# Sparse attention loop: scores five blocks ahead in four PSUM banks, and four buffers of weights

## The reference

```python
logits = jnp.einsum('bthc,btjc->bthj', qb, kv_sel) * (KV_LATENT ** -0.5)
bias = jnp.moveaxis(rel_bias[bucket], -1, 2)
logits = logits + bias.astype(jnp.float32)
logits = jnp.where(valid[:, :, None, :], logits, -jnp.inf)
p = jax.nn.softmax(logits, axis=-1).astype(x.dtype)
o = jnp.einsum('bthj,btjc->bthc', p, kv_sel)
```

## Time and profile before

| What | us |
|---|---|
| median of 3 runs | 3218.07 |
| profiled execution | 3217.28 |
| its span | 3215.4 |
| busy TensorE matmul | 2917.2 (91%) |
| busy VectorE | 1410.9 (44%) |
| busy ScalarE | 920.1 (29%) |
| busy GpSimd | 608.5 (19%) |

### The profile page before, as it was taken

How to read it: one execution, slowest core, us unless ns; L and a number is a source line. 1 busy time by engine, 2 the same in 40 slices (tenths; PEclk the granted TensorE clock), 3 DMA queues, 4 the chain that set the end, 5 groups by cost and what they waited for, 6 DMA issues and landing times.

```text
span 3215.4 us, 42405 instructions
## 1 busy us (share of the span) xinstructions
PE 2917.2 (91%) x17555; PEld 2265.1 (70%) x17555; DVE 1410.9 (44%) x2428; ACT 920.1 (29%) x1696; POOL 608.5 (19%) x534
## 2 busy tenths in 40 slices
PE   8999999999999999999997988888698897988884
PEld 7659999998888778887875555555576674555552
DVE  5635323343345543234444543332597744533234
ACT  4544313233223342232222111111336621211111
POOL 2404101120011220012001432222000003522220
PEclk9999999999999999999998999999899998999997
DMA  4012232222222222222216999999421119999996
GB/s 138 27 53 80 79 105 80 92 79 70 79 70 79 79 78 98 95 96 79 92 53 258 395 409 409 409 408 390 151 88 47 50 60 383 406 409 409 409 409 267
DMA packets 272212, 600.31 MB, mean 187 GB/s; under 512 B 32647, under 2 KB 177602, under 8 KB 255626
## 3 DMA queue, kind: packets, MB, share of 16 engines
q1 hardware_dynamic: 247552, 569.47, 47.1%
q0 software_dynamic: 23968, 27.93, 2.7%
q10 hardware_dynamic: 490, 0.08, 0.0%
HBM read 607.75 MB, written 39.89 MB: 201 GB/s over the span
## 4 chain that ended last, share of the span: by engine, by line
PE 82%; DVE 7%; DMA 4%; issue 4%; ACT 2%; SPq 1%; POOL 1%; ACTq 0%; DVEq 0%; POOLq 0%
PE ps L101 76%; PE ps L104 5%; DMA sb_ring<-in_exp_w_dram 1%; DVE sb_tmpA L118 1%; DVE sb_arena L126 1%; DMA sb_hx<-in_exp_w_dram 1%; DMA sb_arena<-in_exp_w_dram 1%; DVE sb_ws L118 1%; SPq L144 1%; DVE sb_tmpA L126 1%; DVE sb_arena L118 1%; POOL sb_arena L118 0%; DMA sb_arena<-x_rows,sb_smallu 0%; DVE sb_tmpA L2204 0%; DVE sb_tmpA L122 0%
## 5 line engine op out<-in xcount | busy, mean ns | idle before, releaser
L101 PE MATMUL ps<-sb_hs,sb_ws 128*128 128x264 f32 (+1 forms) x6384 | 1106.7, 335 | 17.2 <-ACT sb_hs L108 7.5
L101 PEld LDWEIGHTS ps<-sb_hs,sb_ws 128*128 128x128 f32 x6384 | 971.3, 190 | 148.0 <-issue 16.5
L118 DVE TENSOR_TENSOR sb_ws<-sb_ring,sb_ws 128x1024 fp32r<-128x1024 f32 x279 | 370.6, 1333 | 429.1 <-ACT sb_ws L112 428.6
L101 PE MATMUL ps<-sb_arena 128*64 128x256 f32 (+14 forms) x2052 | 376.5, 429 | 36.7 <-issue 29.7
L112 ACT CAST sb_ws<-sb_ring 128x1024 fp32r<-128x1024 f32 x279 | 290.9, 1046 | 333.0 <-PE ps L101 318.1
L101 PE MATMUL ps<-sb_ring,sb_arena 128*64 128x256 f32 (+2 forms) x2314 | 318.6, 430 | 57.5 <-issue 53.8
L101 PE MATMUL ps<-sb_br,sb_ws 128*128 128x264 f32 (+1 forms) x2304 | 367.4, 321 | 0.0
L101 PEld LDWEIGHTS ps<-sb_br,sb_ws 128*128 128x128 f32 x2304 | 332.4, 188 | 34.2 <-issue 0.5
L101 PEld LDWEIGHTS ps<-sb_arena 128*64 128x64 f32 (+4 forms) x2052 | 220.5, 158 | 154.2 <-issue 88.3
L101 PEld LDWEIGHTS ps<-sb_ring,sb_arena 128*64 128x64 f32 (+1 forms) x2314 | 192.5, 146 | 149.4 <-issue 85.9
L108 ACT ACTIVATE sb_arena<-ps 64x256 f32<-64x256 f32 (+6 forms) x188 | 73.8, 403 | 780.9 <-PE ps L101 758.3
(11 more groups left out here) (189 smaller groups left out, 2265.1 us busy)
## 6 DMA issues: line engine op xcount, KB each, us to landing
sb_ring<-in_exp_w_dram SPq DMA_DIRECT2D x160, 1024.0 KB, 21.2
sb_hx<-in_exp_w_dram SPq DMA_DIRECT2D x128, 1024.0 KB, 21.5
sb_arena<-in_exp_w_dram SPq DMA_DIRECT2D x96, 1024.0 KB, 21.3
sb_ring<-in_mlp_w_dram SPq DMA_DIRECT2D x64, 1024.0 KB, 5.1
sb_ring<-in_od_w_in_dram SPq DMA_DIRECT2D x24, 1024.0 KB, 5.3
sb_ring<-in_conv_w_in_dram SPq DMA_DIRECT2D x12, 1024.0 KB, 5.0
sb_ring<-in_attn_w_in_dram SPq DMA_DIRECT2D x10, 1024.0 KB, 5.2
sb_ring<-in_od_w_out_dram SPq DMA_DIRECT2D x8, 1024.0 KB, 4.8
```

Source lines behind the costliest of these rows:

```text
L101: return self.e.matmul(o, l, r, start=start, stop=stop, skip_group_check=True)
L118: return self.e.tensor_tensor(o, a, b, op)
```

## The change

TensorE gets a ring of four banks for scores (0, 1, 6 and 7) and makes the scores of block x + 5 in step x. VectorE makes scores and maximum of block x + 3, and ScalarE its exponent, in step x, while reciprocal, scaling, transposes and copy still belong to x + 1 and the product to x. The weights get four separate buffers, places 0, 1, 2 and 5 of `tmpA` (3 and 4 stay `PTd`), and `soft_cols` four sets. The loops of ScalarE and VectorE start at x = -3 as before, TensorE's at -5.

```diff
-        P, PTd = tmpA[:, 0:3, 0:512], tmpA[:, 3:5, 0:512]
+        PB, PTd = [tmpA[:, i, 0:512] for i in (0, 1, 2, 5)], tmpA[:, 3:5, 0:512]
...
-            kb, tb, ob = (Ring([BANK[i], BANK[i + 1]], U_, emptied) for i in (0, 2, 4))
-            for x in range(-3, 64):
-                if x + 3 < 64:
-                    h, r = (x + 3) // 4, (x + 3) % 4
+            kb = Ring([BANK[i] for i in (0, 1, 6, 7)], U_, emptied)
+            tb, ob = (Ring([BANK[i], BANK[i + 1]], U_, emptied) for i in (2, 4))
+            for x in range(-5, 64):
+                if x + 5 < 64:
+                    h, r = (x + 5) // 4, (x + 5) % 4
                     n = 128 * (r + 1)
-                    u = kb.take(e, ("ds", x + 3))
+                    u = kb.take(e, ("ds", x + 5))
...
-                        q = e.tp(u[:, 128 * j:128 * j + 128], P[:, (x + 1) % 3, 128 * j:128 * j + 128], ident)
+                        q = e.tp(u[:, 128 * j:128 * j + 128], PB[(x + 1) % 4][:, 128 * j:128 * j + 128], ident)
...
-                if 0 <= x + 2 < 64:
-                    r = (x + 2) % 4
-                    p = P[:, (x + 2) % 3, 0:128 * (r + 1)]
-                    mx, den, inv = soft_cols(x + 2)
-                    e.wait_ge(*dve_dsa["max", x + 2])
+                if x + 3 < 64:
+                    r = (x + 3) % 4
+                    p = PB[(x + 3) % 4][:, 0:128 * (r + 1)]
+                    mx, den, inv = soft_cols(x + 3)
+                    e.wait_ge(*dve_dsa["max", x + 3])
...
-            c = 192 + 4 * (x % 3)
+            c = 192 + 4 * (x % 4)
...
-                    e.wait_ge(*scored["dsa", x + 2])
+                    e.wait_ge(*scored["dsa", x + 3])
                     e.wait_ge(*tb_in[h % 4][h])
-                    if x + 2 >= 3:
+                    if x + 3 >= 4:
                         e.wait_ge(*turned["dp", x - 1])
...
-                    p = P[:, (x + 1) % 3, 0:128 * ((x + 1) % 4 + 1)]
+                    p = PB[(x + 1) % 4][:, 0:128 * ((x + 1) % 4 + 1)]
```

More of the change, by code:

```diff
@@ L2030, in dsa_pe @@
                     e.mm(u[:, 0:n], oT[h][:, 128 * r:128 * r + 128], ckvT[:, 0:n], True, True).then_inc(
-                        *scored.mark(("dsa", x + 3)))
+                        *scored.mark(("dsa", x + 5)))
                 if 0 <= x + 1 < 64:
@@ L2098, in dsa_act @@
             for x in range(-3, 64):
-                if 0 <= x + 2 < 64:
-                    r = (x + 2) % 4
-                    p = P[:, (x + 2) % 3, 0:128 * (r + 1)]
-                    mx, den, inv = soft_cols(x + 2)
-                    e.wait_ge(*dve_dsa["max", x + 2])
-                    e.act(mx, mx, ACT.Identity, scale=-1.0).then_inc(*act_dsa.mark(("less", x + 2)))
-                    e.wait_ge(*act_dsa["less", x + 2])
-                    e.act(p, p, ACT.Exp, bias=mx, acc=den).then_inc(*act_dsa.mark(("exp", x + 2)))
+                if x + 3 < 64:
[3 more added lines that the diff above has]
+                    e.wait_ge(*dve_dsa["max", x + 3])
+                    e.act(mx, mx, ACT.Identity, scale=-1.0).then_inc(*act_dsa.mark(("less", x + 3)))
+                    e.wait_ge(*act_dsa["less", x + 3])
+                    e.act(p, p, ACT.Exp, bias=mx, acc=den).then_inc(*act_dsa.mark(("exp", x + 3)))
                 if 0 <= x + 1 < 64:
@@ L2191, in dsa_dve @@
                     split_lo(e)
-                if 0 <= x + 2 < 64:
-                    h, r = (x + 2) // 4, (x + 2) % 4
+                if x + 3 < 64:
+                    h, r = (x + 3) // 4, (x + 3) % 4
                     n = 128 * (r + 1)
-                    p = P[:, (x + 2) % 3, 0:n]
-                    mx, den, inv = soft_cols(x + 2)
-                    e.wait_ge(*scored["dsa", x + 2])
+                    p = PB[(x + 3) % 4][:, 0:n]
+                    mx, den, inv = soft_cols(x + 3)
+                    e.wait_ge(*scored["dsa", x + 3])
                     e.wait_ge(*tb_in[h % 4][h])
-                    if x + 2 >= 3:
+                    if x + 3 >= 4:
                         e.wait_ge(*turned["dp", x - 1])
-                    e.stt(p, U_["ds", x + 2][:, 0:n], SC128, backwards(TB[:, h % 4, 0:n]), ALU.mult, ALU.add).then_inc(
-                        *dve_emptied.mark(("ds", x + 2)))
-                    e.wait_ge(*dve_emptied["ds", x + 2])
+                    e.stt(p, U_["ds", x + 3][:, 0:n], SC128, backwards(TB[:, h % 4, 0:n]), ALU.mult, ALU.add).then_inc(
+                        *dve_emptied.mark(("ds", x + 3)))
+                    e.wait_ge(*dve_emptied["ds", x + 3])
                     e.e.tensor_tensor_reduce(p, p, madd[:, r, 0:n], 1.0, SENT, ALU.add, ALU.max, mx).then_inc(
-                        *dve_dsa.mark(("max", x + 2)))
+                        *dve_dsa.mark(("max", x + 3)))
                 if 0 <= x + 1 < 64:
-                    p = P[:, (x + 1) % 3, 0:128 * ((x + 1) % 4 + 1)]
+                    p = PB[(x + 1) % 4][:, 0:128 * ((x + 1) % 4 + 1)]
                     mx, den, inv = soft_cols(x + 1)
```

## The result

The changed kernel takes 3195.85 us (median of 4 runs, 3194.71 to 3196.09), beside 3218.34 us for the kernel before: a ratio of 0.993, with a 95% interval of 0.9912 to 0.9947. The profiled execution took 3195.65 us, its span is 3193.9.

What follows compares the result with a forecast made beforehand. Bound: VectorE and TensorE taking turns in the steady loop, 7.15 us a head. Savings of 18.2 us over 14 laps, 1.5 at the start and 2.0 at the end, together 21.7 off 3218.07, gave 3196.4; range 3191 to 3208.

Steps and rivals of the forecast that it cites:

- The bound: Steady loop before: VectorE and TensorE take turns, 7.15 us a head; TensorE's transposes of r=2 wait 1.3 us for scaled weights.
- VectorE's own time, 5.72: Steady loop: what VectorE needs for one head if it never waits, 7.15 us less idle time, reciprocal's wait and overlaps.
- TensorE's own time, 5.68: Steady loop: what TensorE needs for one head if it never waits, 5.46 us plus 0.22 for the last pair.
- The ring through ScalarE, 5.74: Once a head: product r=3, output copy, exponent, copy r=1, product r=1; 2.94 us on ScalarE's side, 2.80 on TensorE's.
- 5.85 a head: Steady loop after the change: 5.74 us plus three hand-offs of about 0.04, bounds 5.74 and 6.3.
- Rival B: Steady loop: limits don't mesh, each block pays a 0.14 us hand-off, 6.3 a head, 3203.2 us; chance 0.18.
- Rival C: Loop and its start: 5.74 us a head and a start at full clock, 3193.4 us; chance 0.12.
- The start, 1.5 between 0 and 3: Start of the loop: 1.5 us saved, as block 3's scores come before TensorE's idle time, at full clock.
- The end, 2.0: End of the loop: the last two outputs copied 4.7 us apart instead of 6.67, saving 2.0 us.
- What follows keeps the gain: After the loop: projection and expert weights move with the loop's end, so nothing swallows the 21.7 us.
- The bias tiles: GpSimd's loads for head h+4: land 1.9 to 5.0 us after issue, needed 17 us later, so hidden.
- rival E: Loop: slower, TensorE's clock stays at 1.2 GHz from the start on, 11.2 us a head, 3279 us; chance 0.04.

Runs made afterwards that it cites:

- e2: The changed kernel with two score banks instead of four and scores made four blocks ahead instead of five: 3211.25 us, ratio 0.998.
- e1: The kernel before with only TensorE's part of the change, four score banks and scores five blocks ahead: 3205.62 us, ratio 0.9963.
- e11: The changed kernel with its four score banks kept but scores made four blocks ahead: 3208.91 us in one run.
- e4: The changed kernel with ScalarE's copy of a head's output moved behind the next step's exponent and copy: 3192.94 us, ratio to before 0.9924.
- e12: The changed kernel with scores made six blocks ahead instead of five, in the same four banks: 3195.86 us in one run, 5.71 us a head.
- e6: The changed kernel with VectorE's two weight splits made before the loop instead of in steps 0 and 1: 3191.68 us, ratio to before 0.9922.
- e3: The changed kernel with three weight buffers instead of four: 3238.0 us, ratio 1.0066.

## Why the prediction was right

- **The bound.** Right. The chain of before was this ring: e2, which leaves one block between making and reading scores as it was, keeps it at 6.85 us. That its 1.3 us of TensorE's idle time come from scores "just made" is borne out by e1, which moves scores alone and takes 0.80 off a head and leaves 0.7 of the 1.3, and by e11, in which banks without distance take nothing off e2's head. The sign that TensorE's waits for the scaling fall below 0.1 us holds for its matmul rows, which show none, but weight loads still wait up to 0.3 us for it.
- **VectorE's own time, 5.72.** Right to 0.01: e4 and e12 both settle at 5.72 a head with only VectorE in their chains. Subtracting idle time and then the overlaps of unwaited successors was worth the trouble; without the overlaps it would have been 6.0.
- **TensorE's own time, 5.68.** Too high by 0.2, without consequence. It was added up from transposes that had waited, and those handed TensorE on later than unwaited ones: two, three and four of them after 0.28, 0.39 and 0.50 us in the rows of before, and after 0.21, 0.33 and 0.43 without a wait. After the change the head is 5.79, less the 0.19 that product r=1 starts late and the 0.11 that it then takes longer: 5.49. So VectorE and the ring lay close together, TensorE did not.
- **The ring through ScalarE, 5.74.** Right in its path, and to 0.04 in size: 2.94 on ScalarE's side as added up, 2.84 instead of 2.80 on TensorE's. There two differences cancel in part. Product r=1 waits now and hands on after 0.55 us (2473.84 to 2474.39; 0.44 before), and the transposes of r=3 don't wait now and hand on after 0.43 (0.50 before). Shown by taking pieces out of it in two places (e4 the output copy, e12 two units of scores), each of which brought the head to VectorE's time.
- **5.85 a head.** 0.06 too much: three hand-offs of 0.04 were added to the ring, and it came out 0.04 above its sum. Times 14 that is, with the shorter last lap, the 1.0 us by which the middle of the loop beat the forecast. Rival B (each block pays 0.14) didn't come: in 2450 to 2480 VectorE shows no wait for TensorE at all. Rival C (5.74 and a full clock) lay nearer in the head than the forecast, but its clock fell.
- **The start, 1.5 between 0 and 3.** 1.9, inside the bounds; that it lies near the middle is luck, for 1.5 was taken without terms of its own. The clock fell later and for less time: the change's clock is 0.69 in 2424 to 2426, 0.50 in 2426 to 2428 and 0.96 in the next two; that of before is 0.56 in 2422 to 2424, 0.50 to 2432 and 0.88 behind it. That scores are made ahead of the idle time, that the second scaling comes later (0.27 us for the 0.35 added up) and that TensorE has little to do until then (2.17 us idle) were seen beforehand. What I did not ask is why the two splits stand there, while VectorE idles for 6 us ahead of the loop: e6 has 3 us from it.
- **The end, 2.0.** 1.8, with 4.86 between the last two outputs for 4.7.
- **What follows keeps the gain.** Right: the first expert weights are issued 23.73 us earlier (2614.74 for 2638.47), the loop's gain of 22.9 and the 1.0 by which it began earlier, less 0.2. Of the 2.4 us that the two profiles lose behind it, the medians show little (0.4).
- **The bias tiles.** Right: nobody waits for them, with 3.4 us to landing.
- **The rules weighed.** By the rule of the Trainium skill (Perfetto Trace Analysis, Optimization Strategy) that consistent bubbles can mean too few buffers, the head would have gone to TensorE's 5.68. The trace after agrees with the place, the 1.31 us are gone; the head stays 0.11 above that figure because the ring sets it. And buffers alone did nothing here: e11 with four banks and e2 with two both take 6.85 us a head, until scores are made one block further ahead. The rule of the Trainium skill on cycling through PSUM banks (TensorE: Matmul & The Clock Gate, A second HAM failure mode: psum-queue depth-cycling), which stood for rival E, is not borne out: with eight banks in rotation the granted clock of the steady loop is 1.00.

## What to carry to other kernels

Where engines hand blocks round in fixed orders, write down each ring that closes once a period, with what stands between two of its members on every engine, and each engine's own time as its waited time less the idle time and less the overlaps that waits had destroyed. The largest is the new period, here to 0.05 us (5.74 for 5.79, and in e4 5.72 for 5.72). An item that nobody is in a hurry for (the output copy) is dear if it stands inside a ring, and a large block can be moved out of it by choosing how far ahead it is made (e12). A bank pays only together with the distance that it is there for (e11 and e2), and a loop that is written for four buffers loses more with three than the whole change had gained (e3, 42 us and 22.5).

## What the runs showed of the hardware that I had not expected

A full-looking TensorE was not the bound: 29.8 of 30 us busy in the change, and e4 and e12 still took 0.07 us off a head, by shortening ScalarE's part of the ring in one and TensorE's in the other. A wait of 0.19 us between matmuls (2473.65 to 2473.84) leaves no idle time in their rows and shows only on the weight loads. And in the change an idle time of 2.17 us, with one transpose and one score matmul between it and an earlier one of 1.19, was followed by the low clock level (0.50 in 2426 to 2428), while one of 1.03 us in the same place in e6 was not (1.00 throughout).
